# Softmax attention by head pairs on row and column groups, with the softmax factor as a row

## The reference

```python
def banded_attention(q, k, v, window, slopes, sink=None):
    ...
    s = jnp.einsum("bnqhgd,bnkhd->bnhgqk", qb, kw).astype(jnp.float32) * Dh ** -0.5
    ...
    s = s - slopes.reshape(Hkv, G, 1, 1) * rel.astype(jnp.float32)
    sk = None if sink is None else sink.astype(jnp.float32).reshape(1, 1, Hkv, G, 1, 1)
    p = masked_softmax(s, mask[None, :, None, None], sk)
    o = jnp.einsum("bnhgqk,bnkhd->bnqhgd", p.astype(v.dtype), vw)
```

## Time and profile before

| | |
|---|---|
| median of 3 runs | 2859.71 us (2854.61 to 2862.65) |
| profiled execution, its own time | 2859.21 us |
| its span, first to last instruction | 2857.2 us |
| mean granted TensorE clock | 0.952 |
| PE busy | 2666.5 us, 93% |
| DVE, ACT, POOL busy | 924.3, 818.3, 874.5 us |
| chain that ended last | PE 87%, DVE 6%, ACT 3%, POOL 2% |

### The profile page before, as it was taken

One profiled execution on the slowest core, in us unless ns is written; L12 is line 12 of the kernel. 1 busy time (PEld: TensorE's weight loads), 2 busy tenths in 40 slices (PEclk: granted clock), 3 DMA queues, 4 the chain that ended last, 5 costly groups with the idle time before them and its releaser, 6 DMA issues.

```text
span 2857.2 us, 30315 instructions
## 1 busy us (share of the span) xinstructions
PE 2666.5 (93%) x12580; PEld 2125.3 (74%) x12580; DVE 924.3 (32%) x1435; ACT 818.3 (29%) x1219; POOL 874.5 (31%) x492
## 2 busy tenths in 40 slices
PE   7799999999998999999998999698999999999896
PEld 4677778666686777787876777487888888888785
DVE  5213430333203544411147465504122222222423
ACT  4103441344322544422222333223211111111321
POOL 2122112444322111144632121244333332333633
PEclk8899999999998988999989999899999999999998
DMA  7001101000011000011221000120111111111111
GB/s 289 32 30 36 38 31 47 28 19 19 17 64 39 11 18 17 8 47 45 102 75 66 16 23 16 35 96 30 46 51 52 45 45 52 52 45 46 56 37 68
DMA packets 34440, 134.84 MB, mean 47 GB/s; under 512 B 3648, under 2 KB 4096, under 8 KB 32896
## 3 DMA queue, kind: packets, MB, share of 16 engines
q1 hardware_dynamic: 33984, 131.85, 13.2%
q10 hardware_dynamic: 320, 1.05, 0.1%
HBM read 123.45 MB, written 8.39 MB: 46 GB/s over the span
## 4 chain that ended last, share of the span: by engine, by line
PE 87%; DVE 6%; ACT 3%; POOL 2%; issue 2%; DMA 1%; POOLq 0%; SPq 0%; ACTq 0%; DVEq 0%
PE slot L659 55%; PE slot L705 12%; PE ps L886 4%; PE ps L857 3%; PE ps L835 2%; PE ps L737 2%; PE ps L919 1%; PE ps L910 1%; PE ps L923 1%; PE ps L936 1%; DVE ada_sum L2035 1%; DVE cacc L2098 1%; PE ps L780 1%; POOL wlo L1499 1%; DMA ada<-wada 1%
## 5 line engine op out<-in xcount | busy, mean ns | idle before, releaser
L659 PE MATMUL slot<-xhi,whi 128*128 128x512 f32 x2192 | 716.3, 409 | 57.7 <-ACT zs L1225 16.8
L659 PE MATMUL slot<-xlo,whi 128*128 128x512 f32 x2192 | 692.3, 398 | 0.0
L659 PE MATMUL slot<-xhi,wlo 128*128 128x512 f32 x2192 | 689.9, 396 | 0.0
L1499 POOL TENSOR_TENSOR wlo<-raw,whi 128x1024 fp32r<-128x1024 f32 (+1 forms) x169 | 429.4, 2541 | 829.7 <-ACT whi L1133 829.7
L659 PEld LDWEIGHTS slot<-xhi,whi 128*128 128x128 f32 x2192 | 406.4, 194 | 147.0 <-issue 65.6
L659 PEld LDWEIGHTS slot<-xlo,whi 128*128 128x128 f32 x2192 | 421.6, 192 | 92.4
L659 PEld LDWEIGHTS slot<-xhi,wlo 128*128 128x128 f32 x2192 | 420.8, 192 | 92.1
L1133 ACT ACTIVATE whi<-raw 128x1024 fp32r<-128x1024 f32 (+1 forms) x169 | 186.1, 1101 | 320.2 <-PE slot L705 174.3
L705 PE MATMUL slot<-uhi,whi 128*128 128x512 f32 x512 | 158.3, 390 | 0.0
L705 PE MATMUL slot<-ulo,whi 128*128 128x512 f32 x512 | 157.8, 389 | 0.0
L705 PE MATMUL slot<-uhi,wlo 128*128 128x512 f32 x512 | 157.6, 389 | 0.0
(11 more groups left out here) (315 smaller groups left out, 3062.2 us busy)
## 6 DMA issues: line engine op xcount, KB each, us to landing
raw<-wstream SPq DMA_DIRECT2D x129, 512.0 KB, 3.2
raw<-wstream SPq DMA_DIRECT2D x40, 640.0 KB, 3.9
ada<-wada SPq DMA_DIRECT2D x7, 1024.0 KB, 19.8
mm<-xT SPq DMA_DIRECT2D x2, 2048.0 KB, 9.7
ada<-wada SPq DMA_DIRECT2D x2, 2048.0 KB, 27.1
mm<-xT SPq DMA_DIRECT2D x8, 512.0 KB, 5.1
res_dram<-mm SPq DMA_DIRECT2D x8, 512.0 KB, 3.0
res<-res_dram SPq DMA_DIRECT2D x8, 512.0 KB, 6.5
```

Source lines behind the costliest of these rows:

```text
L659: o = mm_(outs[:, half * HALF:(half + 1) * HALF], w[b % 2][:, k_w, :], x[:, k_x, half * HALF:(half + 1) * HALF], start=first and j == 0, s ...
L1499: tt(flat(wlo[b % 2])[:, 0:n], (raw1 if b == 1 else raw)[:, 0:n], flat(whi[b % 2])[:, 0:n].bitcast(F32), ALU.subtract).then_inc(w_lo, 1)
```

## The change

The unit of work becomes a pair of heads (t) and a query block: 64 pairs. In SEL, WIN and FGT the query blocks come in the order 0, 7, 1, 6, 2, 5, 3, 4, so that a narrow pair and a wide one (over four key blocks) alternate. A piece is up to four key blocks (512 columns) of a pair.

- `scores`: head 0 of the pair on partitions 0 to 63 into bank `psb[0]`, head 1 on 64 to 127 into `psb[1]`; for each of the three products the two heads follow each other.
- `turn_p(p, a, c)`: the transposes of one head and one piece, through `ps6`; ACT copies to `ptr[:, a, :]`.
- `factor_rows`: the factor of both heads, a column, is spread on PE to a row in `ps7[:, 128:256]` (two matmuls against the identity), and ACT copies it to `frow`.
- `values`: 64 value columns are stationary and the 128 transposed probability columns move; head a goes to partitions 64a to 64a+63 of `ps7[:, 0:128]`. The output is feature-major. DVE multiplies by the row `frow` into `yfm` (and adds, in SEL and WIN).
- `ytrans` falls away for branches B and A (`ymul` on DVE instead) and in `mix`; it stays for C and D.
- The compressed attention writes its outputs feature-major too, in 32 matmuls on 4 row and 2 column groups, with the gate multiplied into the factor. DVE copies them to `yfm`.
- The order is written out by `soft_events`: scores two pairs ahead, put between the transposes of the current pair, and `gap` events for dense work.
- FGT spreads the decay rows of a pair's two heads together, into `cb` and the table `dist`.
- Weights: `cmp` 2 to 1, `pause` 5 to 2.5, `fprep` 2 to 1; the attention steps have none, only their gaps.

```diff
@@
+    if ev[0] == "gap":
+        return ev[1]
+    if ev[0] in ("scores", "bias", "exp", "factor", "frow", "turn_p", "values", "qsplit", "ksplit"):
+        return 0.0
+    if ev[0] == "cmp":
+        return 1.0
...
+    return {"pause": 2.5, "row": 0.7, "fprep": 1.0}.get(ev[0], 2.0)
@@ soft_events
+    out = split(first, first) + split(last + 1, first + 1)
+    for p in (first, first + 1):
+        for c in range(pieces(p)):
+            out += sum(scored(p, c), []) + [("gap", 0.5)]
+        out += split(first + 1, last + 1) + [("exp", first)] if p == first else []
+    out += [("factor", first)] + split(last + 1, first + 2)
+    for p in range(first, last + 1):
+        wide = pieces(p) > 1
+        score, bias = scored(p + 2, 0)
+        out += split(p + 2, last + 1) + [("frow", p), ("turn_p", p, 0, 0)] + score + [("turn_p", p, 1, 0)]
+        out += ([("exp", p + 1)] if p < last else []) + bias
+        factor = [("factor", p + 1)] if p < last else []
+        if wide:
+            score, bias = scored(p + 2, 1)
+            out += [("gap", 1.0), ("values", p, 0), ("turn_p", p, 0, 1), ("gap", 0.5)] + score
+            out += [("turn_p", p, 1, 1)] + bias + factor + [("gap", 0.5), ("values", p, 1)]
+        else:
+            out += [("gap", 1.5)] + factor + [("values", p, 0), ("gap", 1.5)]
+            for c in range(1, pieces(p + 2) if p + 2 <= last else 1):
+                out += sum(scored(p + 2, c), [])
+        out += split(last + 1, p + 3)
@@ TensorE
+            def scores(p, c):
...
+                pe.wait_ge(s_biased, 2 * (PIECE0[p] + c))
...
+                for j, (q_, k_) in enumerate(((q_h, k_h), (q_h, k_l), (q_l, k_h))):
+                    for a in range(2):
+                        r = slice(a * DH, a * DH + DH)
+                        o = mm_(psb[a][:, 0:w], q_[r, :], k_[r, c0:c0 + w], start=j == 0, stop=j == 2)
...
+            def turn_p(p, a, c):
+
+                pe.wait_ge(s_exp, 2 * p + a + 1)
+                pe.wait_ge(s_ptsb, turn_index(p, a, c))
...
+            def factor_rows(p):
+
+                pe.wait_ge(s_fac, p + 1)
+                pe.wait_ge(s_norm, p)
+                for a in range(2):
+                    at_ = 2 * (p % 2) + a
+                    o = mm_(ps7[a * DH:a * DH + DH, P:2 * P], fac[:, at_:at_ + 1].to_broadcast([P, DH]), t_("ident"),
+                            start=True, stop=True)
+                o.then_inc(s_row, 1)
+
+            def values(p, c):
+
+                pe.wait_ge(s_ptsb, turn_index(p, 1, c) + 1)
+                if c == 0:
+                    pe.wait_ge(s_rowsb, p + 1)
...
+                for j in range(n):
+                    for a in range(2):
+                        o = mm_(ps7[a * DH:a * DH + DH, 0:P], value_tile(p, a, b0 + j), ptr[:, a, j * P:(j + 1) * P],
+                                start=b0 + j == 0, stop=b0 + j == pair(p)[4] - 1)
+                o.then_inc(s_out, 1)
@@ ScalarE
+            def turned_p(p, a, c):
+
+                act.wait_ge(s_out, PIECE0[p] + c)
+                act.wait_ge(s_pt, turn_index(p, a, c) + 1)
+                w = piece(p, c)[1] * P
+                nc.scalar.activation(ptr[:, a, 0:w], ps6[:, 0:w], ACT.Copy).then_inc(s_ptsb, 1)
...
+                elif ev[0] == "frow":
+                    act.wait_ge(s_row, ev[1] + 1)
+                    nc.scalar.activation(frow[:], ps7[:, P:2 * P], ACT.Copy).then_inc(s_rowsb, 1)
@@ VectorE
+            def bias(p, c):
...
+                dve.wait_ge(s_scores, PIECE0[p] + c + 1)
+                if p >= 2:
+                    dve.wait_ge(s_pt, turn_index(p - 2, 1, min(c, pieces(p - 2) - 1)) + 1)
...
+                if c == pieces(p) - 1:
...
+                    ins = v.tensor_reduce(nm, ring[p % 2][:, :, 0:nb * P], AX, ALU.max, negate=True)
...
+            def factor(p):
...
+                dve.wait_ge(s_exp, 2 * p + 2)
...
+                ins = v.reciprocal(f, d)
...
+            def outputs(p):
...
+                dve.wait_ge(s_out, PIECE0[p + 1])
...
+                dve.wait_ge(s_rowsb, p + 1)
+                if ph in ("SEL", "WIN"):
+                    link(v.tensor_tensor(frow[:], ps7[:, 0:P], frow[:], ALU.mult))
+                    v.tensor_tensor(y, frow[:], y, ALU.add).then_inc(s_norm, 1)
+                else:
+                    v.tensor_tensor(y, ps7[:, 0:P], frow[:], ALU.mult).then_inc(s_norm, 1)
```

More of the change, by code:

```diff
@@ L120, in spread, with pair, pieces, piece @@
     return out + steps[done:]
[L124 to L130, removed]
[L131 to L156 removed]
+QORDER = (0, 7, 1, 6, 2, 5, 3, 4)
+def pair(p):
+    ph, r = ("SWA", "SEL", "WIN", "FGT")[p // 16], p % 16
+    t, i = r // 8, r % 8 if ph == "SWA" else QORDER[r % 8]
+    lo = {"SWA": max(0, i - 1), "SEL": 0, "WIN": max(0, i - 4), "FGT": 0}[ph]
+    return ph, t, i, lo, i + 1 - lo
+NPAIR = 64
+KTILE = [{"SWA": pair(p)[1], "SEL": 0, "WIN": 1, "FGT": pair(p)[1]}[pair(p)[0]] for p in range(NPAIR)]
+KSPLITS = [p for p in range(NPAIR) if p == 0 or (pair(p)[0], KTILE[p]) != (pair(p - 1)[0], KTILE[p - 1])]
+def pieces(p):
+    return -(-pair(p)[4] // 4)
+PIECE0 = [int(v) for v in np.cumsum([0] + [pieces(p) for p in range(NPAIR)])]
+def piece(p, c):
+    return 4 * c, min(4, pair(p)[4] - 4 * c)
+NRET, NSTICK, NSWA, NSEL, NWIN, NFGT = NB, H * 12, 16, 16, 16, 16
+U_SWA, U_SEL, U_WIN, U_FGT = 0, 16, 32, 48
 STICK = [(h, half, j) for h in range(H) for half in range(2) for j in range(4 * half + 3, -1, -1)]
@@ L171, in soft_events, with split, scored @@
 def soft_events(first, n):
[L172 to L176, removed]
+    last = first + n - 1
+    def split(p, q):
+        return ([("ksplit", p)] if p <= last and p in KSPLITS else []) + ([("qsplit", q)] if q <= last else [])
+    def scored(p, c):
+        if p > last or c >= pieces(p):
+            return [], []
+        rows = [("row", p, a) for a in range(2)] if c == 0 and pair(p)[0] == "FGT" and pair(p)[2] == 0 else []
+        return rows + [("scores", p, c)], [("bias", p, c)]
+    out = split(first, first) + split(last + 1, first + 1)
[19 more added lines that the diff above has]
+        out += split(last + 1, p + 3)
     return out
@@ new lines, in forget_row @@
+            def forget_row(p, a):
+                t = pair(p)[1]
+                if (t, a) == (0, 0):
+                    pe.wait_ge(f_ci, 1)
+                    wait_evacuated(pe, "Ef")
+                pe.wait_ge(s_biased, 2 * PIECE0[p])
+                pe.wait_ge(f_cb, 2 * t + a)
+                h = 2 * t + a
+                for half in range(2):
+                    o = mm_(psb[half], t_("ident")[0:4, h:h + 1].to_broadcast([4, P]),
+                            ct[0:4, half * HALF:(half + 1) * HALF], start=True, stop=True)
+                o.then_inc(f_bc, 1)
```

425 lines of the change are left out of this document (184 added, 241 removed).

## The result

The changed kernel takes 2929.82 us (median of 4 runs, 2927.97 to 2930.88) against 2857.16 us (median of 4, 2854.35 to 2862.65) for the kernel before: ratio 1.0251, 95% interval 1.0233 to 1.0270. It is 2.5% slower; the forecast was 2853, its range ended at 2905.

A forecast was written before the change was run, and what follows sets the result against it. The prediction took PE time (93% busy) plus what makes PE wait as the bound. PE -50, waits -13, clock -15, block boundaries -16, new waits +66, new low clock +22 gave -6 against 2859.2: 2853 us, range 2798 to 2905.

The forecast's parts named there:

- the list of waits that come: New PE waits in the attention stages: wide handovers 58, late exponentials +5, turns at stage ends +3; sum +66 us.
- the clock term: Low clock over the kernel: -15 us regained where waits go, +22 for spells after 13 wide handovers.
- PE's sum: PE time of scores, values, factor rows, mode changes and output turns in the attention stages: net -50 us.
- The mode changes: Entering and leaving half-array groups on PE: 112 more at 0.35 us, +39.2; a rival put 0.6 us each, 2881.
- The weighed rule: Value pairs share all rows, so each of 936 weight loads would show: +50 us; given little chance.
- Waits that go: PE waits in compress, forgetting, last mix and bias rows shrink, sliding window start grows: -13 us; block boundaries -16 besides.
- the sign that no wait there would be over 3 us: Compress stretch: the wait of 6.9 us gone, and waits at most 3 us.
- The block boundaries: Selected and window stretch: PE waits for ACT's sigmoid and lost clock shrink, -16 us, bounds -26 and +15.
- The handover: Wide pairs: the next pair's factor rows wait on PE for DVE's outputs; 58 us over 22 handovers, within the +66.
- The rival in which the clock falls in the wide rounds: Handovers in wide rounds bring 6.8 to 10.2 us of low clock each: 2906 to 2943 us; chance 0.24.
- The chain on DVE: Rival: DVE's handover chain hides, half the 66 us of waits and 22 of clock stay away: 2798 us; chance 0.23.
- Halves: Rival: array halves do not overlap for scores (+43.5 us) or values (+50): about 2900 us; chance 0.05.

The follow-up runs named there:

- the runs with less low clock: Variants of the changed kernel with the same matmuls but less low clock; their PE work at full clock shows 2507 to 2519 us.
- one head after the other: Changed kernel with loops exchanged so all of one head's score and value instructions precede the other head's; 2939.82 us, ratio 1.0294.
- the early split: Changed kernel with the query split of pair p+3 at the head of round p, one round earlier; 2896.34 us, ratio 1.0140.
- filler run: Changed kernel with eight throwaway matmuls behind the last values of wide pairs, in 21 handovers; 2906.26 us, ratio 1.0169.
- both moves: Changed kernel with the query split one round earlier and the factor rows behind turns and scores; 2828.37 us, ratio 0.9900.
- the late rows: Changed kernel with a pair's factor rows behind its two turns and the scores instead of ahead of them; 2874.75 us, ratio 1.0062.

## Why the prediction was wrong

The forecast was 6 us less than before; by the table of work, idle time and clock it became 69 us more. In that table PE's work came out 14 us better than forecast, idle time 54 us worse and the clock 35 us worse. Two steps failed: the list of waits that come had no entry for the query split on POOL (26 us of waits), and the clock term was mis-sized (+7 forecast, +42 measured).

**PE's sum: right in sign and size.** Forecast -50, measured -64 by the table, -52 to -63 from the runs with less low clock. The score line is busy 109 us instead of 184, the value line 74 instead of 125 (0.59 of before for both, where the prediction said half), at the spacing foretold (0.109 us from value pair to value pair). The mode changes were overpriced. From 966.13 to 970.99 stand 4 factor instructions (2 x 0.107), 8 transposes (0.11 each), six scores (3 x 0.23), one dense part (3 x 0.46) and 16 value instructions (8 x 0.107): 4.02 us of streaming in 4.86, so 0.84 for three groups, 0.28 each instead of 0.35. 240 groups at 0.28 in place of 128 at 0.35 are +22 us, not +39.

**The weighed rule: rejecting it was right.** The Trainium skill's page (TensorE: Matmul & The Clock Gate, Part 3, What overlaps and what doesn't) lets a weight load overlap only across row groups. Here sixteen loads and matmuls on shared rows and alternating column halves take 1.02 us; 16 x 0.053 more would have shown. The same section of the Trainium skill has matmuls start strictly in program order. The run with one head after the other shows otherwise: its scores start as khi, khi, brkl, brkl, khi, khi (961.33 to 961.90), where the list has khi, brkl, khi twice.

**Waits that go: -29 forecast, about 10 came.** The compress wait of 6.9 us is gone and the first forgetting wait fell from 8.5 to 2.5 (forecast -4). The bias rows' 3.3 us are gone, and the sliding window start grew from 5.8 to 8.4, as foretold (+2.7). But in the compress stretch a block boundary of 5.0 us came in and the wait for the query split grew from 3.3 to 5.4: its idle time is 14 us as before, and the sign that no wait there would be over 3 us failed. The clock that the prediction took back there (-8 of its -15) did not come either: the stretch went from 0.81 to 0.80. The last mix waits 22.2 us, not less than 20.1. The two copies (1.22 and 1.21 us) did go from DVE's chain, but PE now comes to the wait 2.2 us earlier, since its turns of the outputs are gone, and one operation of that chain (128x1020) took 3.31 us instead of 1.22, beside a split of 2.34 us on POOL. The block boundaries gave 5.5 us over the whole kernel (16.8 to 11.3), and not 16. In the selected and window stretch the prediction took such waits at about 10 us; the trace of before has 6.1 there, and the changed kernel 2.3. The clock that should have come back with them did not.

**The handover: the mechanism right, the size 1.2 times the forecast.** Forecast 66 us; measured 69.3 for outputs ahead of the factor rows and 10.8 ahead of the values, 80 in sum and inside the bound of 1.3 times. Another 6.9 us at the two stage starts the sum had left out. The selected stage's single values (forecast, with the wait ahead of the values in them, 2.0, 3.0, 2.7, 4.6, 3.4, 1.6, 2.7, 1.6) are met by 1.9, 2.4, 2.1, 4.0, 2.5, 1.6, 2.1, 1.5 for the factor rows alone. In the forgetting stage they are higher, 7.4 and 6.7 at the longest, for the short convolution's operations, which the prediction did not look for on DVE. Five convolution steps, which it did name, cost nothing that could be measured. In the window stage, where each was put at 3.0, two took 5.0 and 5.1. POOL has a part in these. On POOL, DVE and PE:

```profile
1173.23 2.88 POOL L1547 TENSOR_TENSOR wlo<-raw,whi 128x1280 fp32r<-128x1280 f32 x1
1173.53 2.73 DVE L1947 TENSOR_TENSOR yfm<-frow,yfm 128x128 f32<-128x128 f32 x1
1176.40 0.69 PE L914 MATMUL ps<-tab,fac 128*64 128x128 f32 x4 [5.11 <-DVE yfm L1947]
```

The output operation, 0.29 us elsewhere, began while POOL's weight split ran and ended 0.1 us after it. The same operation took 2.33 us at 1221.49, beside an operation of 2.34 us on POOL. No run tested this by moving POOL's work.

**A missed wait: the query split on POOL, +26.** This is the first step that failed: the part by part has no entry for the moved split. Before, it was issued a whole unit ahead of its scores, with values and transposes between; in the new order it is the last event of a round, and only the factor rows and one turn stand between it and the scores of the next. Waits of scores for POOL went from 12.2 us (the row of 3.26 in the earlier trace rows is one of them) to 38.2; 4.7 of the difference are the two stage starts told above. The prediction asked for every queue that a moved step passes on DVE and PE, not on POOL, where weight splits of 2.9 us and additions of 2.34 us (line 1605) lie. The run with the early split measures the cause at 33 us with its clock.

**The clock: the term that was mis-sized, +7 forecast, +42 measured.** The forecast gave one spell of 3.4 us for each of 13 handovers. The rival in which the clock falls in the wide rounds took place, and it had the right sign to look for: 0.84 where under 0.88 spoke for 2900. The granted clock in the changed kernel, in three neighbouring stretches and one ahead of them:

```profile
1021.90:1025.30 3.40, 3.39 (x16) 2.79 (x17) 0.46 (x2) 1.32 (x3) 0.00 (x0) 0.50 0.03 5
1039.00:1045.80 6.80, 5.62 (x20) 4.15 (x21) 2.82 (x12) 3.62 (x8) 0.00 (x0) 0.50 0.00 0
1045.80:1052.60 6.80, 4.02 (x23) 2.42 (x21) 1.86 (x4) 2.86 (x5) 2.40 (x2) 1.00 0.00 0
1052.60:1059.40 6.80, 5.55 (x31) 4.14 (x32) 1.28 (x2) 2.97 (x6) 0.35 (x1) 0.50 0.01 2
...
1053.10 0.79 PE L889 MATMUL ps<-khi,qp 64*128 64x512 f32 x2 [3.28 <-POOL qp L1640]
```

The low clock from 1021.9 goes with a handover of 2.07 us, which ended at 1021.4; that from 1039.0 with the handover of 4.00 us and the one from 1052.6 with a wait for POOL of 3.28. In the selected and window stretch and the forgetting stretch 28 such spells begin (8 before). 22 of them go with a wait for outputs, 3 with a wait for POOL and 3 with another wait. The 14 that began after the end of their wait (waits of 1.2 to 2.8 us) lasted 3.4 us each; the 14 that began inside their wait (2.4 to 7.4 us) lasted 6.8, one of them 10.2. Five waits of 1.3 to 2.7 us brought none. So the term was too small in both factors: 22 handovers brought a spell and not 13, and half of the spells were twice as long or more. The filler run (0.84 to 0.92) and the run with both moves (0.93) show the cause by taking the idle time away. The rule cited for this rival, from the Trainium skill (TensorE: Matmul & The Clock Gate, Part 1), agrees with the trace that far. How the 42 us divide can be seen in part: the early split alone takes about 8 us of lost clock away, the late rows alone 32. The rival's time, 2906 to 2943, holds the result; it reached it, though, with part of the POOL waits in its clock. (Its remark that half of the handovers give 2885 names the upper end; its own sum gives 2868 to 2887.)

**The rivals that fell.** The chain on DVE did not hide (69 us of waits). Halves do overlap. The mode change costs less, not more.

## What to carry to other kernels

When a kernel is bound by TensorE, a change that thins its work makes each wait count more than once, as idle time and as half clock behind it (here 91 us of added idle time came with 42 us of added clock loss). So the new order's waits have to be listed on all queues first. An instruction that waits should stand behind everything on its engine that does not need it, and a small operation on a queue that also holds long ones should be issued a round before its reader: these two moves turned 2.5% slower into 1.0% faster, and one dense part ahead of the waiting rows made it 1.6%.

## What the runs showed of the hardware

TensorE does not start matmuls strictly in the order of the program when they lie on different halves of the array. Three fp32r products of one row half ahead of three of the other ran pair by pair (0.91 us, as with the order written out), and of two runs of eight fp32 instructions on column halves the second began when five of the first had started (1.51 against 1.02 us). In these rows alternating the halves by hand gained nothing for groups of three and 0.5 us for groups of eight.

Entering and leaving a group on halves of the array cost 0.28 us where the pairs run side by side, against 0.35 for a group on one row half. The 0.28 is an average over three groups of one round.

An operation of 0.29 us on DVE took 2.73 and 2.33 us when it began while a long operation ran on POOL, and ended within 0.2 us of that one's end.

168 filler matmuls, 47 us of PE work, made the kernel 24 us faster, through the clock (138 to 107 us lost) and the idle time that they stand in.
